# Four expert down matrices per layer loaded in three transfers (112, 8 and 8 partitions) instead of one of 128

## The reference

```
for i in range(DEPTH):                      # DEPTH = 2
    h = mixer_i(x)
    x = layer_norm(ALPHA * x + h, ...)
    f = moe(x, ...)                         # 64 routed experts, top 8 of 64 per token, one shared expert
    x = layer_norm(ALPHA * x + f, ...)
# an expert: y = (silu(h @ w_gate[e]) * (h @ w_up[e])) @ w_down[e]
# w_gate, w_up: 1024 x 256; w_down: 256 x 1024, all float32, 1 MB each
```

## Time and profile before

| | |
|---|---|
| Median of 3 runs | 1292.71 us (1292.02 to 1294.69) |
| The profiled execution's own time | 1291.81 us |
| Its span, first to last instruction | 1290.1 us |
| TensorE's mean granted clock | 0.983 |
| PE busy | 1206.5 us, 94% of the span |
| DVE, ACT, POOL busy | 44%, 29%, 1% |
| Bytes moved by DMA | 473.87 MB, 367 GB/s in the mean |
| Downs in transfers of 1 MB | 126 from line 491, median 24.7 us from issue to landing |

### The profile page before, as it was taken

The page is one execution under the profiler, slowest core; times in us unless marked ns, Lnnn a source line. Parts: engine busy times, 40 slices in busy tenths (PEclk is TensorE's granted clock), DMA queues, the critical chain, the costliest instruction groups (busy, mean ns, idle before and its releaser), DMA issues.

```text
span 1290.1 us, 20270 instructions
## 1 busy us (share of the span) xinstructions
PE 1206.5 (94%) x7916; PEld 735.8 (57%) x7916; DVE 570.6 (44%) x1266; ACT 372.1 (29%) x664; POOL 14.9 (1%) x31
## 2 busy tenths in 40 slices
PE   9999999999888888989999999999999888888997
PEld 7986444444333444559999998544444444334454
DVE  6756443333323223328676766634233333233233
ACT  4443222222112222315554444222222221122230
POOL 0001000000000000000000000000000000000000
PEclk9999999999999999999999999999999999989899
DMA  9977999999999999999735436899999999999995
GB/s 302 388 301 318 390 419 416 411 420 421 421 421 421 420 420 421 421 411 400 270 130 195 165 139 244 329 415 415 422 408 421 420 421 421 420 420 421 421 420 229
DMA packets 92338, 473.87 MB, mean 367 GB/s; under 512 B 8145, under 2 KB 23633, under 8 KB 46417
## 3 DMA queue, kind: packets, MB, share of 16 engines
q1 hardware_dynamic: 90176, 469.79, 90.0%
q10 hardware_dynamic: 2064, 2.75, 0.6%
HBM read 471.46 MB, written 1.05 MB: 366 GB/s over the span
## 4 chain that ended last, share of the span: by engine, by line
PE 63%; DMA 25%; SPq 6%; DVE 4%; issue 1%; ACT 1%; POOL 0%; DVEq 0%; ACTq 0%
DMA ring<-in_w_up 20%; PE ps L887 19%; PE ps L767 10%; PE ps L938 7%; PE ps L779 6%; PE ps L809 5%; SPq L491 4%; PE ps L866 4%; PE ps L955 3%; PE ps L977 2%; PE ps L899 2%; DMA ring<-in_w_gate 2%; DMA ring<-in_w_down 2%; PE ps L985 1%; SPq L527 1%
## 5 line engine op out<-in xcount | busy, mean ns | idle before, releaser
L887 PE MATMUL ps<-ring,xsT 128*32 128x512 f32 (+1 forms) x2048 | 330.2, 628 | 52.1 <-DMA ring<-in_w_up 52.0
L887 PEld LDWEIGHTS ps<-ring,xsT 128*32 128x32 f32 (+1 forms) x2048 | 105.2, 125 | 268.4 <-issue 267.0
L938 PE MATMUL ps<-ring,hidT 128*32 128x512 f32 (+1 forms) x1200 | 189.7, 596 | 4.1 <-DMA ring<-in_w_down 4.1
L1636 DVE SCALAR_TENSOR_TENSOR sig<-sig,slot_gate,ps 128x256 f32<-128x256 f32 x52 | 25.0, 480 | 365.1 <-ACT sig L1296 365.1
L1433 DVE TENSOR_TENSOR ring_low<-ring,wh 128x1024 fp32r<-128x1024 f32 (+1 forms) x111 | 128.2, 1155 | 87.1 <-ACT wh L1220 86.2
L1220 ACT CAST wh<-ring 128x1024 fp32r<-128x1024 f32 (+1 forms) x111 | 109.5, 988 | 151.2 <-PE ps L767 60.9
L1659 DVE TENSOR_TENSOR X<-X,ps 128x512 f32<-128x512 f32 x184 | 118.2, 682 | 51.8 <-PE ps L955 37.1
L1296 ACT ACTIVATE sig<-ps 128x256 f32<-128x256 f32 x52 | 20.0, 384 | 402.5 <-PE ps L887 349.5
L1650 DVE TENSOR_TENSOR yl<-ps,yh 128x512 fp32r<-128x512 f32 x104 | 71.5, 690 | 130.5 <-ACT yh L1305 130.5
L1284 ACT ACTIVATE xsT<-ps,cols 128x256 f32<-128x256 f32 x208 | 101.8, 560 | 82.8 <-PE ps L866 82.8
L938 PEld LDWEIGHTS ps<-ring,hidT 128*32 128x32 f32 (+1 forms) x1200 | 52.8, 119 | 101.7 <-issue 101.0
(11 more groups left out here) (208 smaller groups left out, 1384.0 us busy)
## 6 DMA issues: line engine op xcount, KB each, us to landing
ring<-in_w_gate SPq DMA_DIRECT2D x128, 1024.0 KB, 20.3
ring<-in_w_down SPq DMA_DIRECT2D x126, 1024.0 KB, 24.7
ring<-in_w_up SPq DMA_DIRECT2D x124, 1024.0 KB, 22.4
ring<-in_b_w_in SPq DMA_DIRECT2D x8, 3072.0 KB, 26.0
ring<-in_b_w_out SPq DMA_DIRECT2D x4, 3072.0 KB, 10.9
ring<-in_a_w_in SPq DMA_DIRECT2D x9, 1024.0 KB, 12.1
ring<-in_w_up SPq DMA_DIRECT2D x8, 512.0 KB, 24.5
ring<-in_a_w_out SPq DMA_DIRECT2D x1, 3072.0 KB, 18.9
```

The costliest lines, as they stand in the source:

```text
L887: last = nc.tensor.matmul(ps[first:first + width, p, :], xsT[:, c, p * P + first:p * P + first + width], gate_up_of(layer, k, c), start=(c ...
L938: last = nc.tensor.matmul(ps[first:first + width, 4 + h, :], hidT[:, p, kk * P + first:kk * P + first + width], down_of(layer, k)[:, kk, h ...
```

## The change

The downs of experts E-9, E-8, E-7 and E-6 of each layer are no longer loaded in one transfer of 128 partitions. They are loaded in three: partitions 0 to 111, then 112 to 119, then 120 to 127. All three add 16 to the same semaphore, and `down_ready` counts two more transfers for each such down, so PE still waits for the whole matrix. Nothing else is changed: the bytes, their order on the queue and all of PE's, DVE's and ACT's instructions are the same. Eight downs of 128 are concerned, four in each layer, and SP issues 16 transfers more.

```
+SPLIT_DOWNS = (E - 9, E - 8, E - 7, E - 6)
...
-    return 16 * (loads_of(layer, k) - elsewhere)
+    split = sum(1 for l in range(DEPTH) for n in SPLIT_DOWNS if slot_of(l, n) == s and (l, n) <= (layer, k))
+    return 16 * (loads_of(layer, k) - elsewhere + 2 * split)
...
             def load_down(layer, k, expert):
                 s = slot_of(layer, k)
-                load_matrix(layer, s, expert, w_down, HC, GU, dn_load[s])
+                if k not in SPLIT_DOWNS:
+                    load_matrix(layer, s, expert, w_down, HC, GU, dn_load[s])
+                    return
+                src = w_down[layer, bass.ds(expert, 1)].rearrange("e (p c) n -> (e p) (c n)", c=HC)
+                for first, last in ((0, P - 16), (P - 16, P - 8), (P - 8, P)):
+                    sp.dma_start(ring[first:last, s, GU:SLOT], src[first:last]).then_inc(dn_load[s], 16)
```

## The result

The changed kernel takes 1328.37 us in the median (1327.22 to 1331.55, 4 runs), the kernel before 1292.44 us beside it. The ratio is 1.0273, with a 95% interval of 1.0261 to 1.0285: about 35 us or 2.7% slower. The forecast was 1294.1 us, the range ended at 1298.7.

A forecast was written before the change was run, and what follows sets the result against it. The prediction took the stream of 1 MB transfers to bound both layers' ends; imbalance of +0.7 us a layer, +1.4 us in all, with other terms at 0, on the 1292.71 us median gave 1294.1 us, range 1290.8 to 1298.7.

The forecast's parts named there:

- What bounds the kernel: Ends of both routed stages: the stream of 1 MB transfers ends last, and any delay to it shows in full.
- main step: Split downs' packets over the engines: eight carry 9, eight carry 7; +0.7 us a layer, +1.4 us for both.
- rival 2: Split downs' odd shapes run below the packet rate: +5.0 us, 1297.7 us, 7 us or more if packets hinder; chance 0.24.
- The small transfers' own cost: 8-partition transfers: a packet costs 0.313 us wherever written, the lower end; upper end, packets one behind the other, +35 us.
- The imbalance: In each split down eight engines carry 9 packets and eight 7: up to 1.25 us later at each layer's end.
- The bound by ten late engines: Layer 1's stream end: some ten engines are late and eight relieved, so at least two late ones get more.
- The windows before the last landing of layer 1: Sign in 1 us windows there: fewer engines idle before the down lands, as those ahead carry 4 packets more.
- SP's issues at zero: Eight more issues a layer, 2.6 to 7.4 us of SP's time, hidden by the queue: cost 0.
- The users of the split downs: Units 22 and 23: their downs land 5.4 and 7.6 us before use, so a microsecond's delay costs nothing.

The follow-up runs named there:

- relieving the upper eight: Against the kernel before: E-9 and E-8 load their second half of columns only to partitions 0 to 63, in eight strided transfers; 1292.09 us, ratio 0.9988.
- the one of 112 and 16: Against the kernel before: the same eight downs loaded in two transfers, of 112 and 16 partitions; 1321.55 us, ratio 1.0222.
- 8 neighbours and every fourth partition: Against the kernel before: E-9's second half of columns in 16 transfers of 8 partitions, neighbouring (1300.38 us) or every fourth of a block of 32 (1300.68 us).
- a narrow source with a whole target: Against the kernel before: eight downs in two transfers, each reading 64 neighbouring rows and writing all 128 partitions; 1293.10 us, ratio 1.0003.
- a spread source with a narrow target: Against the kernel before: eight downs in two transfers, each reading every second row and writing 64 neighbouring partitions; 1325.16 us, ratio 1.0258.

## Why the prediction was wrong

**What bounds the kernel: right.** The stream of 1 MB transfers ends last, and what it loses shows in full: 36.1 us of deficit in the two stretches, 39.7 us of time in the same execution, 35 us by the ratio of all. The prediction's own sign against its main step came true: it named 417 GB/s or below as the mark of rival 2, and the rate was 277 and 246 GB/s.

**The step that failed** is "The small transfers' own cost", in the words "a packet costs 0.313 us wherever it is written". Packets took 0.479 us in the mean over 50 us. I had the two ends, 0 and +35 us, and took the lower one because the nearest row was the ordinary packet rate. But the rows it rests on the earlier trace rows came from transfers of 128 partitions. They could not say anything about another shape, and so were not near to it at all. That the upper end equals the measured loss is chance: it was worked out for small transfers on one engine each, and they run on eight, and the large piece carries most of the loss (29 us alone). In its place the runs show that a packet's time depends on which partitions are written: the stream kept 420 GB/s with 32 to 95 and fell to 313 GB/s with 0 to 63.

**Rival 2** had the kind of mechanism, the odd shapes running below the packet rate, at 0.24, and mis-sized it at 5.0 us ("7 us or more" if the eight hinder each other). It let the piece of 112 take 2.50 us instead of 2.19. Measured, one such down costs 4.4 to 5.6 us, and it slows the full transfers around it. The argument against it, "nothing in the profile shows an engine slowed by another one's target", was true of the trace and worth nothing: there was no such case in it. The range then ended 4.6 us over the forecast, at 1298.7, although a bound of 35 us stood in the text.

**The imbalance**, on which the forecast stood: eight engines for a small transfer is right (127 completion writes more). The bound by ten late engines held where it was tested: relieving the upper eight brings 1.6 us (0.4 to 2.8), of at most 2. The windows before the last landing of layer 1, which the prediction named as its sign, went the other way from what it said, with fewer engines at work and not more. First the changed kernel (down begins at 1313.13 us), then the one of 112 and 16 (1304.28 us):

```profile
1310.00:1311.00 1.00, 1.00 0.59 242
1311.00:1312.00 1.00, 1.00 0.30 123
1312.00:1313.00 1.00, 1.00 0.18 74
```

```profile
1302.00:1303.00 1.00, 1.00 0.63 258
1303.00:1304.00 1.00, 1.00 0.47 188
```

In the last us before the landing 0.18 x 16 = 2.9 engines' worth is at work, where it was 9.4 before. Added up over the last six us, 2.2 us of stream are idle, against 0.8 us in the kernel before and 1.1 us in the one of 112 and 16, which has no imbalance. So some 1.0 to 1.4 us at this layer's end fit the forecast's +1.25 us, from one profiled execution of each. The term was of about the right size and far too small to matter. In time the changed kernel lies 6 to 7 us above the one of 112 and 16, and that difference holds the imbalance and the meeting of small transfers together.

**SP's issues at zero: right**, by the kernel cut in columns (+0.9 us, -0.5 to +2.5). **The users of the split downs: wrong for the first.** 5.4 and 7.6 us were said to be spare. PE now waits 3.76 us before unit 22's down; unit 23's shows no wait, as PE had waited 6.11 us for that unit's up. The spare time was set against a delay of a microsecond, and the delay was many times that.

**What stays open.** That two engines share a group of partitions evenly would give 2.5 us for a down in two halves; measured are 4.1 to 4.7 us. The engines are out of step by some us, so at one time some may be in a split piece and others in the full transfers around it, and each group then has a guest for longer than the piece lasts. That fits the 12 us of slow windows above and the up of E-8, which stood ahead of the split downs and landed 8.5 us after the rate had fallen. But it is argued, not shown. So are the sharing itself, that engines wait for one another at the target, and which engine takes which partitions. Nor was it shown why 8 neighbours and every fourth partition cost the same.

## What to carry to other kernels

Where the stream of loads is the limit, keep each transfer at all 128 partitions and cut it by columns if it must be cut; a cut by columns of the same proportions cost 0.9 us for eight downs here (-0.5 to +2.5), one by partitions 4 to 6 us for each MB. Look at share and GB/s together: a share of 1.01 at 277 GB/s was the sign of slow packets, where the same share had gone with 421 GB/s. And when an operation has a shape that the trace doesn't contain, let the range go to the bound instead of asking for a row that cannot exist.

## What was not expected of the hardware

- The place of a transfer of 64 partitions in SBUF decides its price: partitions 32 to 95 left the stream at 420 GB/s, partitions 0 to 63 brought it to 313 GB/s over 50 us.
- The slow stretch is longer than the split transfers themselves: two halves of 1 MB in all made some 12 us of slow stream and cost 4.7 us.
- The read side made no difference where it was tested: a narrow source with a whole target ran at 418 GB/s, a spread source with a narrow target at 291 GB/s.
